# Routed experts in two tiles at least: weight subtractions on VectorE alone, 1024 wide, and the activation transposed in three groups

## The reference

```python
logits = xt @ router_w + router_b                      # xt: 2048 x 1024
top_vals, top_idx = lax.top_k(logits, 4)
gates = softmax(top_vals)
# each token's row goes to its 4 experts, sorted by expert
gu = ragged_dot(xs, w_gu, group_sizes) + b_gu          # 1024 -> 2048 for each expert
gate = minimum(gu[:, ::2], 7); up = clip(gu[:, 1::2], -7, 7)
act = (up + 1) * (gate * sigmoid(1.702 * gate))
y = ragged_dot(act, w_down, group_sizes) + b_down      # 1024 -> 1024
# rows weighted by the gates and added up for each token
```

## Time and profile before

| what | value |
|---|---|
| runs (3) | 6580.18, 6582.07, 6592.33 us |
| median | 6582.07 us |
| profiled execution | 6574.97 us, span 6573.3 us |
| TensorE / VectorE / ScalarE / GpSimd busy | 5683.1 / 3367.7 / 2243.3 / 1147.0 us |
| mean granted TensorE clock | 0.931 |
| bytes moved by DMA | 730.14 MB, mean 111 GB/s |
| stages, by the trace | mixer to about 1110 us, experts to about 4135 us, the rest behind |

### The profile page before, as it was taken

The page is one execution under the profiler, slowest core; times in us unless marked ns, Lnnn a source line. Parts: engine busy times, 40 slices in busy tenths (PEclk is TensorE's granted clock), DMA queues, the critical chain, the costliest instruction groups (busy, mean ns, idle before and its releaser), DMA issues. The chain is left out here.

```text
span 6573.3 us, 83382 instructions
## 1 busy us (share of the span) xinstructions
PE 5683.1 (86%) x25368; PEld 3490.0 (53%) x25754; DVE 3367.7 (51%) x6606; ACT 2243.3 (34%) x3821; POOL 1147.0 (17%) x1021
## 2 busy tenths in 40 slices
PE   7999996889989999989999999599979999731978
PEld 3555553555555555555555555355547777631744
DVE  3333433566566666565665565433334444587077
ACT  3111112444344445444453453222223333320043
POOL 0000001233133333232332232000000000140000
PEclk9999997999999999999999999799989999865589
DMA  3000002465366656465563566422320000110033
GB/s 113 23 26 29 19 29 76 155 198 192 120 198 198 201 178 210 151 199 168 175 209 127 164 203 197 160 91 99 104 82 4 7 6 7 41 15 0 29 136 102
DMA packets 381179, 730.14 MB, mean 111 GB/s; under 512 B 75184, under 2 KB 100336, under 8 KB 379760
## 3 DMA queue, kind: packets, MB, share of 16 engines
q1 hardware_dynamic: 322272, 564.49, 26.1%
q10 hardware_dynamic: 33984, 90.19, 3.9%
q0 software_dynamic: 24816, 74.01, 3.6%
HBM read 617.36 MB, written 108.82 MB: 110 GB/s over the span
## 5 line engine op out<-in xcount | busy, mean ns | idle before, releaser
L732 PE MATMUL GU<-w_hi,x_hi 128*128 128x512 f32 x2432 | 1431.9, 589 | 40.8 <-DVEq L1014 37.0
L924 ACT ACTIVATE w_hi<-stage 128x512 fp32r<-128x512 f32 x1536 | 918.1, 627 | 447.1 <-DMA stage<-in_expert_w_down_dram 205.0
L884 POOL TENSOR_TENSOR w_lo<-stage,w_hi 128x512 bf16<-128x512 f32 x576 | 777.0, 1370 | 1312.6 <-ACT w_hi L924 1305.2
L733 PE MATMUL GU<-w_hi,x_lo 128*128 128x512 f32 x2432 | 962.2, 396 | 0.0
L734 PE MATMUL GU<-w_lo,x_bf 128*128 128x512 bf16 x2280 | 901.1, 395 | 0.0
L991 DVE TENSOR_TENSOR w_lo<-stage,w_hi 128x512 bf16<-128x512 f32 x960 | 673.6, 753 | 242.3 <-ACT w_hi L924 241.2
L732 PE MATMUL Y<-w_hi,a_hi 128*128 128x512 f32 x1216 | 718.9, 591 | 59.1 <-DVE a_lo L1002 59.1
L602 PE MATMUL PJ<-w_in_sb,xT 128*128 128x512 f32 x1280 | 575.2, 603 | 41.9 <-ACT w_in_sb L370 31.5
L734 PEld LDWEIGHTS GU<-w_lo,x_bf 128*128 128x128 bf16 x2432 | 236.0, 97 | 672.5 <-issue 672.5
L732 PEld LDWEIGHTS GU<-w_hi,x_hi 128*128 128x128 f32 x2432 | 495.8, 204 | 48.2 <-DVEq L1014 43.7
L733 PEld LDWEIGHTS GU<-w_hi,x_lo 128*128 128x128 f32 x2432 | 469.5, 193 | 62.6
(11 more groups left out here) (499 smaller groups left out, 8970.9 us busy)
## 6 DMA issues: line engine op xcount, KB each, us to landing
stage<-in_expert_w_gate_up_dram SPq DMA_DIRECT2D x1024, 256.0 KB, 4.8
stage<-in_expert_w_down_dram SPq DMA_DIRECT2D x512, 256.0 KB, 4.9
expert_rows<-acted ACTq DMA_DIRECT2D x76, 512.0 KB, 2.7
b_gu<-in_expert_b_gate_up_dram ACTq DMA_DIRECT2D x128, 256.0 KB, 4.3
b_d<-in_expert_b_down_dram ACTq DMA_DIRECT2D x32, 512.0 KB, 8.6
z<-z_sb SPq DMA_DIRECT2D x16, 992.0 KB, 8.4
w_in_sb<-in_w_in_dram SPq DMA_DIRECT2D x8, 1280.0 KB, 15.7
expert_rows<-zero_rows SPq DMA_DIRECT2D x20, 512.0 KB, 6.9
```

The lines of the kernel that those rows point to most:

```text
L732: pe.matmul(out, high(k), w_high(k), start=(k == first), stop=False)
L733: pe.matmul(out, low(k), w_high(k), start=False, stop=False)
L884: pool.tensor_tensor(w_lo[:, c, ks, :], stage[:, m % STAGES, :, :], w_hi[:, c, ks, :], ALU.subtract).then_inc(s["lo_pool"], 1)
L924: act.activation(w_hi[:, c, weights_of(m)[1], :], stage[:, m % STAGES, :, :], ACT.Copy).then_inc(s["hi_done"], 1)
```

## The change

1. Each expert has at least two tiles (L563 of before: max with 2), so each has a last tile and at least one before it. The loops take `n_more` tiles and then the last, for the 32nd expert also. The result buffer grows from 96 to 128 tiles; its upper 64 are filled with zeros in the mixer phase, a sixteenth in every tile.
2. Units are 128 x 2 x 512 (512 KB), 24 for an expert, in a stage of 4 slots of the same size together. All subtractions are on VectorE, 1024 wide. 13 (`HEAD`) stand in the last tile, in an order written out by hand; the other 11 stand behind that tile's result.
3. `acted` is transposed in three groups, 4, 2 and 2 blocks (`A_PARTS`), and the `down` products follow in that order; the gathered rows are transposed later in the tile. x_hi and x_lo are one instruction each, 1024 wide.

```diff
-            ch.link(dve.tensor_scalar(cnt[:, :], cnt_i[:, :], 1.0, None, ALU.max))
+            ch.link(dve.tensor_scalar(cnt[:, :], cnt_i[:, :], 2.0, None, ALU.max))
...
                 sp.dma_start(hn_t[bass.ds(t, 1)].squeeze(0), hn_sb[:, :]).then_inc(s["hn_stored"], 16)
+                sp.dma_start(unused[bass.ds(t, 1)].squeeze(0),
+                             zero_y[:, :].unsqueeze(1).to_broadcast([P, 2 * E // TILES * KD, P])).then_inc(s["y_zeroed"], 16)
                 if has_x:
                     sp.wait_ge(s["h_stored"], t * 16 + 16)
                     load_x(t + 2, par)
...
-MAX_TILES = SEQ * TOPK // P + E
+MAX_TILES = SEQ * TOPK // P + 2 * E
...
-PARTS = 8
-DVE_PARTS = 5
-KP = KD // PARTS
-ALL_PARTS = PARTS * CHUNKS_W
-STAGES = PARTS
+KP = 2
+STAGES = 4
+UNITS = [(c, part) for c in range(GU_CHUNKS) for part in range(4)] + [
+    (GU_CHUNKS + n, part) for parts in ((0, 1), (2,), (3,)) for n in range(2) for part in parts]
+N_UNITS = len(UNITS)
+HEAD = 13
+A_PARTS = (slice(0, 4), slice(4, 6), slice(6, 8))
```

ScalarE in the last tile of an expert, n being the next (`high` copies a unit to w_hi; VectorE's `last` has `low` of the same units in the same places):

```diff
+            def last(e, g, n):
+                if n is None:
+                    return body(e, g)
+                act.wait_ge(s["gu_ps"], g * GU_CHUNKS + 1)
+                high(n, 0)
+                tanh_of(g, 0)
+                bias(n, 0)
+                high(n, 1)
+                high(n, 2)
+                act.wait_ge(s["gu_ps"], g * GU_CHUNKS + 2)
+                high(n, 3)
...
+                a_high(g, 2)
+                x_high(g + 1)
+                high(n, 11)
+                high(n, 12)
+                store(g)
+                bias_down(n)
+                for m in range(HEAD, N_UNITS):
+                    high(n, m)
```

TensorE's second half of a tile:

```diff
-                pe.wait_ge(s["a_ready"], g * 4 + 2)
-                down(0, 0)
-                transpose_rows(g + 1)
-                transpose_act(g, 1)
-                down(1, 0)
-                pe.wait_ge(s["a_ready"], g * 4 + 4)
-                down(0, 1).then_inc(s["y_half"], 1)
-                down(1, 1).then_inc(s["y_ps"], 1)
+                pe.wait_ge(s["a_ready"], g * 6 + 2)
+                transpose_act(g, 1)
+                pe.wait_ge(s["y_taken"], g + 1)
+                down(0, 0)
+                down(1, 0)
+                pe.wait_ge(s["a_ready"], g * 6 + 4)
+                down(0, 1)
+                transpose_act(g, 2)
+                down(1, 1)
+                transpose_rows(g + 1)
+                pe.wait_ge(s["a_ready"], g * 6 + 6)
+                down(0, 2)
+                down(1, 2).then_inc(s["y_ps"], 1)
```

More of the change, by code:

```diff
@@ L795, in expert_phase, with experts, before_last, place @@
         half = BANK // 2
-        def experts(eng, body, last_body):
+        def experts(eng, body, last):
             def read(table, e, most):
                 return eng.value_load(S[table][0:1, bass.ds(e, 1)], min_val=0, max_val=most)
+            def before_last(e):
+                start = read("starts", e, MAX_TILES - 1)
+                with eng.Fori(0, read("n_more", e, CAP_T - 1)) as t:
+                    body(e, eng.snap(start + t, min_val=0, max_val=MAX_TILES - 1))
             with eng.Fori(0, E - 1) as e:
[L803 to L827, removed]
+                before_last(e)
+                last(e, read("last", e, MAX_TILES - 1), e + 1)
+            before_last(E - 1)
+            last(E - 1, read("last", E - 1, MAX_TILES - 1), None)
+        def place(m):
+            c, part = UNITS[m]
+            return c, slice(part * KP, part * KP + KP)
         @block.sync
@@ L876, in gather, with rest @@
                 pool.sem_inc(s["ids_free"], 1)
[L878 to L889, removed]
             def read(table, e, most):
                 return pool.value_load(S[table][0:1, bass.ds(e, 1)], min_val=0, max_val=most)
-            def gathers(e):
-                first = read("starts", e, MAX_TILES - 1)
+            def rest(e):
+                start = read("starts", e, MAX_TILES - 1)
                 with pool.Fori(0, read("n_more", e, CAP_T - 1)) as t:
-                    gather(e * CAP_T + t + 1, pool.snap(first + t + 1, min_val=0, max_val=MAX_TILES - 1))
+                    gather(e * CAP_T + t + 1, pool.snap(start + t + 1, min_val=0, max_val=MAX_TILES - 1))
+            gather(0, 0)
             with pool.Fori(0, E - 1) as e:
[L901 to L905, removed]
+                rest(e)
+                gather(e * CAP_T + CAP_T, read("starts", e + 1, MAX_TILES - 1))
+            rest(E - 1)
             total = pool.value_load(S["starts"][0:1, E:E + 1], min_val=0, max_val=MAX_TILES)
@@ L918, in bias_down, with high @@
                 act.dma_start(b_d[:, :], b.partition_broadcast(P)).then_inc(s["bd_in"], 16)
[L920 to L925, removed]
+            def high(e, m):
+                c, ks = place(m)
+                act.wait_ge(st_in[m % STAGES], (e * (N_UNITS // STAGES) + (m // STAGES + 1)) * 16)
+                act.activation(w_hi[:, c, ks, :], stage[:, m % STAGES, :, :], ACT.Copy).then_inc(s["hi_done"], 1)
@@ L943, in body @@
[L943 to L959 removed]
+                ks = A_PARTS[n]
@@ L970, in _ @@
             bias_down(0)
-            split(0, 0)
+            for m in range(2):
+                high(0, m)
             x_high(0)
-            for c in range(1, CHUNKS_W):
-                split(0, c)
-            experts(act, body, lambda e, g: body(e, g, e + 1))
+            for m in range(2, N_UNITS):
+                high(0, m)
+            experts(act, body, last)
             total = act.value_load(S["starts"][0:1, E:E + 1], min_val=0, max_val=MAX_TILES)
@@ new lines, in swiglu @@
+            def swiglu(e, g, c):
+                dve.wait_ge(s["tanh_ready"], g * GU_CHUNKS + (c + 1))
+                ch.link(dve.scalar_tensor_tensor(gate[:, :], tanh[:, :], 1.0, gate[:, :], ALU.add, ALU.mult))
+                if c == 0:
+                    dve.wait_ge(s["y_stored"], g * 16 + 16)
+                dve.scalar_tensor_tensor(acted[:, c * half:(c + 1) * half], up[:, :], 1.0, gate[:, :],
+                                         ALU.add, ALU.mult).then_inc(s["acted_ready"], 1)
```

260 lines of the change are left out of this document (138 added, 122 removed).

## The result

The changed kernel took 6875.94 us (median of 4 runs, 6868.85 to 6879.96), the kernel before 6582.69: a ratio of 1.0442, 95% interval 1.0423 to 1.046. The direction was right; +293 us stand against a forecast of +172, and the time lies 6 us beyond the range. The profiled execution took 6879.96 us, span 6878.1.

A forecast was written before the change was run, and what follows sets the result against it. TensorE, busy 86% of the span, with the expert phase largest and 35.05 us the floor of a tile. Profiled 6575 + 122 (mixer zeros) + 50 (first tiles) = 6747 us; range 6590 to 6870.

The forecast's parts named there:

- Zeros hold x: Mixer: x's load waits behind 2 MB of zeros on SP's queue, 14 loads x 8.7 us = 122 us lost.
- Rival A: Mixer: x is not held by the zeros, so the 122 us go: 6625 us; chance 0.12.
- the 20 copies: End of the expert phase: 512 KB zero writes behind the last weights; what they gave way to was costed at nothing.
- at most 320 GB/s: Mixer zeros: trace's top rate, set beside the 358 GB/s estimate of 5.9 us a piece; 7.2 us was taken.
- The last tile: Last tile of an expert: falls to about the floor of 35.05 us; 0 to 0.3 us a tile, taken as 0.
- The first tile: Next expert's first tile: TensorE stands 9.6 us behind eleven subtractions; excess 11.6 against 10.0 us a pair, 50 us lost.
- a slot's round is 6.5 us, so 1.6 us a unit: Next expert's first tile: pace of subtractions 13 to 23 through four stage slots, the 23rd ending at 23.4 us.
- rival C: Next expert's first tile: tail at 2.0 us a unit (262 GB/s), excess 15.3 us, 6861 us; chance 0.14.
- Rival B: Next expert's first tile: loads keep ahead, tail at VectorE's pace, excess 4.8 us, gain 161, 6536 us; chance 0.13.
- the stretched instructions: Last tile: VectorE steps slowed beside GpSimd's subtractions, up 1.38 us against 0.29 alone, go away entirely.

The follow-up runs named there:

- the move: The changed kernel with SP's 2 MB of zeros put behind the load of x in each mixer tile: 6741.99 us, ratio 1.0253.

## Why the prediction was right in sign and too small

A walk over kernels that ran adds up the whole change, in ratios to the kernel before and in us of 6576. All subtractions on VectorE: 1 to 0.9819, -119 us. Then 1024 wide units in four slots and their new order, with the tail in the first tile and the zeros behind x, but two groups: 0.9822, +2, in which several effects may cancel. Three groups: 0.9589, -153. The tail in one piece behind the result: 1.0253, +437. The zeros ahead of x: 1.0442, +124. The two losses, 561 us, exceed the two gains, 272, and with the +2 the sum is +291.

1. **Zeros hold x: right, a little small.** The wait was 6.9 us against the 6.8 forecast, which is partly luck: the bytes cost x 6.7 us (10.6 less 3.9) where 7.2 was taken, and x was issued 1.42 us behind hn instead of 0.63, which the forecast left out. The clock took some 2.3 us against 1.9, and 14 such tiles make 128 us for 122. Rival A is refuted by the move (124 us) and by the zeros in the kernel before (+121 us with nothing else changed). The first result is 138 us late, 7 of them behind the mixer, where the forecast had no term. At the other end, what the 20 copies gave way to was rightly put at nothing: from the last result to the end it takes 2442.5 us before and 2444.4 now. The rule of the Trainium skill, "DMA: Bandwidth & Descriptors" (Queues, rings and completion order), that descriptors of one issuing queue are consumed in ring order on each DMA engine, agrees with the landing of 10.6 us behind 2 MB, 7.5 behind 1 MB, 4.1 behind none. That the trace has "at most 320 GB/s" holds for the stretch of the copies alone; the earlier trace rows has 385 GB/s.
2. **The last tile: right.** It fell from 47 to 38.4 us in the median, 35.05 plus the 3.0 us by which its result is taken later; no wait on x, and 0.7 us a pair in front of the transposes, most of it on acted.
3. **The first tile: mechanism right, size wrong.** This is the step that failed: "a slot's round is 6.5 us, so 1.6 us a unit". It measured 7.7 us, 1.9 a unit. In the example unit 13 ends at 7.5 us (forecast 7.1), 17 at 15.6 (13.6) and 23 at 26.6 (23.4): (26.6 - 7.5) / 10 = 1.9 us a unit. The landing was taken as 3.9 us from a lone load of 512 KB, though half that size took 5.1 in the ring; in the ring it is 5.4 here and 5.8 by the median of the `down` pieces. The bank comes at 28.9 (26.1), TensorE asks for it at 17.0 (16.5) and stands 11.9 (9.6); the mean over 31 is 12.3. With the 0.7 us in front of the transposes and 2.3 left, for the clock above all (2.0), the excess is 15.3, rival C's number, though not for C's reason: C had the rate of bytes (262 GB/s), while the experiments with 256 KB units and three slots show a ring that leaves the DMA engines partly idle. 31 x (15.3 - 11.6) = 115 us, nearly all of the 121 (293 less 172) that were missed.
4. **Rival B** would have needed loads that keep ahead. VectorE waited 372.6 us in the phase for ScalarE's copies, and ScalarE 402.9 for the stage. That the change could have gained was right, but by another way: the order, not the pace.
5. **GpSimd.** The prediction counted the stretched instructions as gone, and they are (`up` 0.29 by the mean of all). What it did not see is that this alone, without fewer or wider subtractions, is worth 119 us: VectorE with 48 subtractions an expert keeps up better than with 30 and GpSimd beside it. The time that VectorE got back lies mostly in its gates, which TensorE awaits for the transposes; how much of the 119 comes from there and how much from slots that are free sooner stays open. Of that kernel too I expected a loss (6640), and it gained.

Open: why a load of 512 KB lands in 5.4 to 5.8 us in the ring and in 4.1 alone, while the share is below 1 for much of it. Fewer in flight land sooner (4.8 to 4.9 with three slots), and so do the `down` pieces when the tail is spread over the first tile (4.8, through the same four slots); no run took a single landing apart.

## What to carry to other kernels

A row of work put behind a result in one piece costs the engine that needs the next step all of it, however idle that engine's supplier is on average; laid between the next tile's steps the same work cost 437 us less here. Take a load's duration from a ring like the one in which it will run: a lone load's 3.9 us in place of 5.4 to 5.8, 31 times over, was most of what this forecast missed. And a store nobody waits for belongs behind the load somebody waits for, on a queue that serves both.

## What the runs showed of the hardware

- The issue of x by SP, behind 2 MB of zeros in 512-byte pieces, held SP for 5.88 us instead of 0.36; behind 1 MB in such pieces, and behind 2 MB in pieces of 1 KB, 2.4 us each. So an issuing engine can be held by its queue's backlog, and here the hold went by the number of pieces (4096 against 2048), while the landing of x went mostly by the bytes (10.6 and 9.6 us behind 2 MB, 7.5 behind 1 MB).
- A 3.7 us wait of TensorE cost about as much in granted clock as one of 6.9 us, some 2.3 us a time (the granted clock was 0.50 in the 4 us behind either).
- A load of 256 KB lands in 4.7 to 5.2 us and one of 512 KB in 5.4 to 5.8 in the same ring: halving it hardly shortens the landing, and more slots in turn are what helps. With three slots of 512 KB the median is 4.8 to 4.9.
- VectorE's result addition, w_lo at 1024 columns and x_lo all take 1.22 us; three w_lo in a row 3.50, so 1.17 each, near the 1.15 forecast.
